# Sixteen experts on one core: 32x32 block turns on VectorE in place of turns on TensorE

## The chip, the cores and the metric

One Trainium2 chip, of which the kernel uses one core. The metric is device microseconds of one execution. All times of the profile are microseconds from the start of its span unless marked ns.

## The reference

One layer over 128 context rows and 512 latent rows, each 1024 wide: a modulated RMSNorm, a mixer (a convolution half and a bidirectional gated linear attention half), an output projection, and then a mixture of experts with a final RMSNorm. The change lies in the mixture, which is:

```python
def _ec_moe(h, w_router, w_gate, w_up, w_down):
    Bn, T, _ = h.shape
    cap = EC_CAPACITY_FACTOR * T // N_EXPERTS          # 64 latent rows, 16 context rows
    probs = jax.nn.softmax((h @ w_router).astype(jnp.float32), axis=-1)
    gates, idx = lax.top_k(jnp.swapaxes(probs, 1, 2), cap)
    xs = h[bidx, idx]
    a = jax.nn.silu(einsum(xs, w_gate)) * einsum(xs, w_up)
    y = einsum(a, w_down) * gates[..., None]
    return jnp.zeros_like(h).at[bidx, idx].add(y)
```

There are 16 experts. Each has three weights of 1024 x 1024 float32 (12.6 MB an expert, 201 MB in all), and takes 64 latent and 16 context rows. Here h is the norm of x2 times (1 + scale2) plus shift2, with one scale and shift for latent rows and one for context rows; then x = x2 + gate2 * mixture, and the final norm. Everything is float32.

## The kernel before

The mixer runs in the first 340 us or so. Then comes the loop over the experts, `expert(e, k)` with k = e on each engine, on which this case turns.

**Weights.** SP (the sync engine) loads each expert in six transfers of 2 MB: u0 and u1 are the first halves of gate and up (512 of the 1024 input rows), u2 and u3 their second halves, u4 and u5 the halves of down. They go through a ring of nine slots (`load_rows`, L552). Transfer n = 6e + u waits until TensorE has used transfer n - 9 (`load_later`, L561: `gu_used` counts two for each expert, `d_used` two). All of them stand in one queue of SP.

**Rows.** POOL gathers an expert's 80 rows of the normalised h from DRAM into `xs` (L675, two buffers) and adds the results of an expert to `sum_l` and `sum_c` in DRAM by indirect DMAs with addition (`add_rows`, L683). The rows of the normalised h are stored so that column j of group kk is input row 4 x partition + j of a weight half.

**TensorE**, for an expert, in this order (L2254): the gate and up products of the 64 latent rows (L2275, `gate_ps` and `up_ps`; it waits for u0 and u1 before the first half and for u2 and u3 before the second, then for the tokens `xT`); the first half of the gate and up products of the 16 context rows (L2305, `ctx_ps`; the pad of 16 columns goes with them); `turn_latent_products` (L2290: the 128x512 tile `act_l` turned in four 128x128 turns into PSUM); the second half of L2305; the latent down products, first half (L2320); `turn_context_products` (L2296: four turns); `turn_tokens(e + 1)` (L2234: the 80x1024 tile `xs` of the next expert in eight turns into pair 2 of PSUM); the second half of L2320; the context down products (L2333).

**ScalarE** takes SiLU of the gate products (L1108 latent, L1112 context) and then brings the turned latent tokens of the next expert from PSUM to `xT` with scale and shift (L1094, eight instructions). **VectorE** multiplies by the up products (L1703, L1710), copies the turned products from PSUM to `aT` (L1706) and `aTc` (L1716), brings the context tokens to `xT` (L1692, L1694), and scales the results into `y_l` and `y_c` (L1698).

**The first expert** has its tokens turned on TensorE in an order of its own (`turn_first_rows`, `first_tokens`).

**The last expert and the end.** While the last expert runs, SP reloads the sums of the other fifteen into `x_sb` (L596, five tiles; the queue is that of the weights). ScalarE squares tiles 0 to 3 (L1103), then does the context SiLU (L1112), loads a table, squares tile 4 and takes the roots (L1120). VectorE, in the order of its program, multiplies tiles 0 and 1 by the gain (`gain_rows`), multiplies `act_c` (L1710), waits for the roots and inverts them (`inverse_after`, L1157 to L1162), copies `aTc` (L1716), finishes rows (`finish_rows`, L1762 and L1765), and only then scales `y_l` (L1698), adds what the other experts left (L1742), and so on. TensorE stops before its last eight context down products for `last_sum_of(0)` (L2251), which needs the squares of that `y_l` (L1135). The last chain goes from `y_c` through L1742, the inverse and L1752 to two scattered stores (L716, L721).

Of the kernel before, what the change touches and what calls it, by code (L numbers as in the profile page):

```python
# [22 lines left out]
ALU = mybir.AluOpType  # L23
# [183 lines left out]
def build(nc, x_prompt, x_sample, s_fwd, s_bwd, c, c_ctx, w_mod, b_mod, g_norm1, g_norm2, w_in, w_conv, b_conv,  # L207
# [3 lines left out]
    with ctx:  # L211
# [9 lines left out]
        def small(name, shape, dt=F32):  # L221
# [86 lines left out]
        xs = at("xs", B_XS, [SLOTS, 2, D])  # L308
# [49 lines left out]
            pool_chain gu_used dl_done d_used xTp_done xT_lat xT_ctx xT_zero gul_done silu_lat silu_ctx act_l_ready  # L358
            act_c_ready aTp_l aTp_c aT_ready aTc_ready yl_ready yc_ready yl_added yc_added sums_in
# [9 lines left out]
         act_chain, pool_chain, gu_used, dl_done, d_used, xTp_done, xT_lat, xT_ctx, xT_zero, gul_done, silu_lat, silu_ctx,  # L369
         act_l_ready, act_c_ready, aTp_l, aTp_c, aT_ready, aTc_ready, yl_ready, yc_ready, yl_added, yc_added, sums_in,  # L370
# [236 lines left out]
        def _(pool):  # L607
# [60 lines left out]
            def gather_first():  # L668

                pool.wait_ge(idx_ready, 2)  # L670
                pool.wait_ge(hn_out[0], 48)
                g.indirect_dma_start(xs[CAP_L:SLOTS, 0, :], None, hn[:, :],
                                     bass.IndirectOffsetOnAxis(ap=first_ctx[0:CAP_C, 0:1], axis=0)).then_inc(xs_ctx, 16)

            def gather(e):  # L675
                if e >= 2:
                    pool.wait_ge(xTp_done, e - 1)
                    pool.wait_ge(xTc_done, 1)
                g.indirect_dma_start(xs[:, e % 2, :], None, hn[:, :],
# [46 lines left out]
        def _(act):  # L726
# [379 lines left out]
            def expert(e, k):  # L1106
                act.wait_ge(gul_done, e + 1)
# [6 lines left out]
                if k < E - 1:  # L1114
                    tokens(e + 1, k + 1)
                else:
# [25 lines left out]
        def _(dve):  # L1142
# [505 lines left out]
            v.memset(xT[:, :, :, SLOTS:96], 0.0).then_inc(xT_zero, 1)  # L1648
# [7 lines left out]
            v.tensor_copy(selr[:, 2, :], pad_rows[:, :])  # L1656
            c = slice(NT - 1, NT)
# [26 lines left out]
            def tokens(e, k):  # L1684
                dve.wait_ge(xT_lat, e + 1)
                if e == 0:
                    dve.wait_ge(xTc_done, 1)
                src = pairs[2][:, :].rearrange("p (b n) -> p b n", b=2)[:, :, 0:4 * SLOTS].rearrange(
                    "p b (k s) -> p b k s", s=SLOTS)[:, :, :, CAP_L:SLOTS]
                dst = xT[:, k % 2, :, CAP_L:SLOTS].rearrange("p (b k) s -> p b k s", b=2)  # L1690
                by = lambda ap: ap.rearrange("p (b k) v -> p b k v", b=2).to_broadcast([P, 2, 4, CAP_C])
                v.tensor_tensor(dst, src, by(scale2[:, :, 1:2]), ALU.mult).then_inc(xT_ctx, 1)  # L1692
                dve.wait_ge(xT_ctx, 2 * e + 1)
# [680 lines left out]
```

## Time and profile before

| | |
|---|---|
| median of 3 runs | 889.68 us (889.63 to 889.81) |
| span of the profiled execution | 889.4 us |
| TensorE (PE) busy | 867.2 us, 98% |
| VectorE (DVE) busy | 286.5 us, 32% |
| ScalarE (ACT) busy | 229.0 us, 26% |
| data moved | 272.39 MB, mean 306 GB/s |

The profiled execution has no time of its own beside its span; the span lies 0.3 us under the median of the runs. In rows of `--timeline` kind the columns are: start, duration (from the first start to the last end of the instructions merged), engine, line, operation, output<-input, shapes, count, and in brackets the idle time before and who ended it. SPq and POOLq are the queues of issues of these engines.

### The profile page before, as it was taken

How to read it: one execution, taken by the hardware profiler on the slowest of the kernel's cores; microseconds unless marked ns; L12 is line 12 of the kernel's file. 1: busy time of each engine (PE TensorE's matmuls, PEld its weight loads, DVE VectorE, ACT ScalarE, POOL GpSimd, SP SyncE). 2: the span in 40 equal slices, each digit the busy share in tenths (PEclk: the TensorE clock that was granted, in tenths of full speed). 3: DMA queues.
4: the chain of work that ended last, by engine and by line, in shares of the span. 5: the costliest groups of instructions: out<-in, count | busy, mean ns of one | idle time of the engine just before them, and what ended most of it. 6: DMA issues, size and time to landing. Idle time of an engine off the chain costs nothing.

```text
span 889.4 us, 14543 instructions
## 1 busy us (share of the span) xinstructions
PE 867.2 (98%) x6341; PEld 480.7 (54%) x6341; DVE 286.5 (32%) x610; ACT 229.0 (26%) x451; POOL 83.2 (9%) x83
## 2 busy tenths in 40 slices
PE   6999999999999999999999999999999999999995
PEld 5798899989998875333333333333333333333332
DVE  3576544777465574201101101101101101101123
ACT  5566634462351333101101101101101101101114
POOL 1000000000000021111011011011011011011013
PEclk9999999999999999999999999999999999999998
DMA  9864714523148358999999999999999999999973
GB/s 329 279 220 165 278 65 136 192 96 134 69 157 349 123 206 303 375 384 410 397 383 412 402 382 409 402 384 409 403 383 415 397 383 412 400 382 410 422 259 135
DMA packets 52770, 272.39 MB, mean 306 GB/s; under 512 B 6378, under 2 KB 16654, under 8 KB 40420
## 3 DMA queue, kind: packets, MB, share of 16 engines
q1 hardware_dynamic: 44908, 255.15, 73.1%
q0 software_dynamic: 6128, 10.89, 5.2%
q10 hardware_dynamic: 1672, 5.43, 1.5%
q8 instruction: 50, 0.82, 0.4%
q14 instruction: 12, 0.10, 0.0%
HBM read 257.95 MB, written 14.55 MB: 306 GB/s over the span
## 4 chain that ended last, share of the span: by engine, by line
PE 91%; DVE 3%; DMA 3%; ACT 1%; SPq 1%; issue 1%; POOLq 0%; POOL 0%; DVEq 0%
PE pair L2275 25%; PE pair L1892 15%; PE pair L2320 13%; PE pair L2305 13%; PE pair L2333 6%; PE pair L2131 5%; PE pair L1832 2%; PE pair L1927 2%; DMA scale_b<-in_w_mod 2%; PE pair L2234 1%; PE pair L2290 1%; DMA p1w<-in_w_out 1%; PE pair L2059 1%; PE pair L2296 1%; PE pair L2050 1%
## 5 line engine op out<-in xcount | busy, mean ns | idle before, releaser
L2275 PE MATMUL pair<-ring,xT 128*64 128x512 f32 x1024 | 223.9, 594 | 0.3 <-ACT xT L1086 0.3
L2275 PEld LDWEIGHTS pair<-ring,xT 128*64 128x64 f32 x1024 | 71.9, 137 | 142.1 <-issue 141.9
L2305 PE MATMUL pair<-ring,xT 128*32 128x512 f32 x1024 | 116.5, 595 | 0.9 <-DVE xT L1694 0.9
L2320 PE MATMUL pair<-ring,aT 128*64 128x512 f32 x512 | 116.9, 598 | 0.0
L1108 ACT ACTIVATE act_l<-pair 128x512 f32<-128x512 f32 x16 | 9.6, 597 | 290.8 <-PE pair L2275 290.8
L1703 DVE TENSOR_TENSOR act_l<-act_l,pair 128x512 f32<-128x512 f32 x16 | 11.0, 687 | 207.9 <-ACT act_l L1108 207.9
L1892 PE MATMUL pair<-hT_hi,w_hi 128*128 128x320 f32 x320 | 75.9, 319 | 0.0
L1892 PE MATMUL pair<-hT_lo,w_hi 128*128 128x320 f32 x320 | 73.1, 310 | 0.0
L1892 PE MATMUL pair<-hT_hi,w_lo 128*128 128x320 f32 x320 | 72.9, 309 | 0.0
L2320 PEld LDWEIGHTS pair<-ring,aT 128*64 128x64 f32 x512 | 34.0, 136 | 69.5 <-issue 68.2
L2305 PEld LDWEIGHTS pair<-ring,xT 128*32 128x32 f32 x1024 | 30.2, 109 | 73.1 <-issue 73.1
L687 POOL DMA_INDIRECT sum_l<-y_l,row_l x15 | 23.4, 1559 | 393.3 <-DVE y_l L1698 393.3
L2333 PE MATMUL pair<-ring,aTc 128*32 128x256 f32 x1024 | 58.8, 381 | 0.0
L1892 PEld LDWEIGHTS pair<-hT_hi,w_hi 128*128 128x128 f32 x320 | 53.0, 188 | 5.7 <-issue 3.9
L1892 PEld LDWEIGHTS pair<-hT_lo,w_hi 128*128 128x128 f32 x320 | 53.7, 188 | 0.0
L1892 PEld LDWEIGHTS pair<-hT_hi,w_lo 128*128 128x128 f32 x320 | 53.7, 188 | 0.0
L1094 ACT ACTIVATE xT<-pair,mod,scale 128x64 f32<-128x64 f32 x120 | 37.2, 412 | 60.9 <-PE pair L2234 60.9
L2333 PEld LDWEIGHTS pair<-ring,aTc 128*32 128x32 f32 x1024 | 31.5, 110 | 32.1 <-issue 13.0
L1234 DVE TENSOR_TENSOR w_lo<-p1w,w_hi 128x1024 fp32r<-128x1024 f32 (+1 forms) x33 | 29.9, 930 | 25.1 <-ACT w_hi L795 24.9
L1112 ACT ACTIVATE act_c<-pair 64x512 f32<-64x512 f32 x16 | 9.4, 589 | 108.8 <-PE pair L2305 108.8
L2131 PE MATMUL pair<-wo_hi,yT_hi 128*128 128x512 f32 x80 | 32.5, 406 | 0.0
L2131 PE MATMUL pair<-wo_hi,yT_lo 128*128 128x512 f32 x80 | 31.6, 395 | 0.0
(307 smaller groups left out, 933.0 us busy)
## 6 DMA issues: line engine op xcount, KB each, us to landing
ring<-in_w_gate SPq DMA_DIRECT2D x32, 2048.0 KB, 30.3
ring<-in_w_up SPq DMA_DIRECT2D x32, 2048.0 KB, 19.4
ring<-in_w_down SPq DMA_DIRECT2D x32, 2048.0 KB, 25.1
p1w<-in_w_mod SPq DMA_DIRECT2D x8, 2048.0 KB, 8.3
p1w<-in_w_in SPq DMA_DIRECT2D x5, 2048.0 KB, 8.0
p1w<-in_w_mod SPq DMA_DIRECT2D x7, 1024.0 KB, 12.3
x_sb<-in_x_sample SPq DMA_DIRECT2D x8, 512.0 KB, 4.9
p1w<-in_w_out SPq DMA_DIRECT2D x2, 2048.0 KB, 8.0
```

The costliest lines, as they stand in the source:

```text
L687: g.indirect_dma_start(rows_l, bass.IndirectOffsetOnAxis(ap=row_l[:, e:e + 1], axis=0), y_l[:, e % 2, :], None, compute_op=ALU.add).then_i ...
L1094: ins = a.activation(xT[:, k % 2, kk, 0:CAP_L], xT_ps(kk)[:, 0:CAP_L], ACT.Identity, bias=mod[:, 3 * KC + kk, 0:1], scale=scale2[:, kk, 0:1])
L1234: v.tensor_tensor(w_lo[place][:, rows, tile(j)], p1w[place][:, rows, tile(j)], rounded(name)[:, rows, tile(j)].bitcast(F32), ALU.subtract) ...
L1703: v.tensor_tensor(in_fours(act_l[:, :]), in_fours(act_l[:, :]), up_ps.rearrange("p (q j) -> p j q", j=4), ALU.mult).then_inc(act_l_ready, 1)
L1832: ins = mm(pp[g:g + 32, 0:mod_width(u)], silu_c[:, k, :], w[:, k, :], start=k < 4, stop=k >= 4)
L1892: ins = mm(pp[:, s * 512:s * 512 + HALF], w, h[:, s * HALF:(s + 1) * HALF], start=k == 0 and i == 0, stop=k == KC - 1 and i == 2)
L1927: ins = mm(pp[:, cols], h, w, start=k == 0 and i == 0, stop=k == KC - 1 and i == 2)
L2131: ins = mm(pp[:, half * 512:(half + 1) * 512], y, w, start=k == 0 and i == 0, stop=k == KC - 1 and i == 2)
L2275: ins = mm(ps[64 * n:64 * n + 64, :], xt[:, kk, 0:CAP_L], w[:, j, n * 512:(n + 1) * 512], start=kk == 0, stop=kk == KC - 1)
L2305: ins = mm(ctx_ps[32 * g:32 * g + 32, :], xt[:, kk, CAP_L:96], w[:, j, n * 512:(n + 1) * 512], start=kk == 0, stop=kk == KC - 1)
L2320: ins = mm(y_ps[0][r:r + 64, :], aT[:, j, 64 * fh:64 * fh + 64], wd[:, j, n * 512:(n + 1) * 512], start=fh == 0 and j == 0, stop=fh == 1 a ...
L2333: ins = mm(y_ps[1][32 * b:32 * b + 32, 0:256], aTc[:, j, 32 * fh:32 * fh + 32], down[fh][:, j, 256 * b:256 * b + 256], start=fh == 0 and j ...
```

## The change

- The eight turns of tokens, for experts 1 to 15, and the four and four turns of products, for all experts, leave TensorE. The helper `turned(dst, src, s, n)` on VectorE does them from SBUF to SBUF: four transposes of 32x32 blocks, one for each output quadrant r, each reading the 32 partitions 32s..32s+31 and writing the 32 partitions 32r..32r+31, n blocks in one instruction.
- Tokens: three times `turned(..., KC)`, 12 instructions of 32x256; `aT`: 16 instructions of 32x128; `aTc`: 8 instructions of 32x128. The copies L1706 and L1716 go. The multiplication before each set is now waited for by VectorE itself.
- The tokens of expert e + 1 are made at the start of expert e on VectorE and ScalarE (for 0 < e < 15), and in expert 0 where they were before. ScalarE's eight instructions now work in place on `xT` in SBUF; VectorE's two for the context rows likewise.
- `xs` has 96 rows, and rows 64 to 95 are cleared once on VectorE (a memset of 32 partitions x 2048) before the first context gather; the memset of `xT` covers one buffer in place of two. POOL's gather of e waits for `xs_turned`, of tokens e - 2.

```diff
@@ gather @@
-                if e >= 2:
-                    pool.wait_ge(xTp_done, e - 1)
+                if e == 2:
+                    pool.wait_ge(xTp_done, 1)
                     pool.wait_ge(xTc_done, 1)
+                if e >= 3:
+                    pool.wait_ge(xs_turned, e - 2)
@@ scalar, tokens and expert @@
-                act.wait_ge(xTp_done, e + 1)
+                act.wait_ge(xs_lat, e)
                 for kk in range(KC):
-                    ins = a.activation(xT[:, k % 2, kk, 0:CAP_L], xT_ps(kk)[:, 0:CAP_L], ACT.Identity,
+                    ins = a.activation(xT[:, k % 2, kk, 0:CAP_L], xT[:, k % 2, kk, 0:CAP_L], ACT.Identity,
             def expert(e, k):
+                if 0 < k < E - 1:
+                    tokens(e + 1, k + 1)
                 act.wait_ge(gul_done, e + 1)
@@ vector @@
-            v.memset(xT[:, :, :, SLOTS:96], 0.0).then_inc(xT_zero, 1)
+            v.memset(xT[:, 0, :, SLOTS:96], 0.0).then_inc(xT_zero, 1)
...
+            v.memset(xs[CAP_L:96, :, :], 0.0).then_inc(xs_zero, 1)
...
+            def turned(dst, src, s, n):
+                for r in range(4):
+                    ins = v.transpose(dst[32 * r:32 * r + 32, :, 32 * s:32 * s + 32],
+                                      src[32 * s:32 * s + 32, :].rearrange("p (k r c) -> p r k c", k=n, r=4)[:, r, :, :])
+                return ins
+            def tokens(e, k):
+                dve.wait_ge(xs_full[k % 2], 16 * (e // 2 + 1))
+                if k >= 2:
+                    dve.wait_ge(gu_used, 2 * (e - 1))
+                turned(xT[:, k % 2], xs[:, k % 2, :], 0, KC)
+                turned(xT[:, k % 2], xs[:, k % 2, :], 1, KC).then_inc(xs_lat, 1)
+                turned(xT[:, k % 2], xs[:, k % 2, :], 2, KC).then_inc(xs_turned, 1)
+                dve.wait_ge(xs_turned, e)
...
             def expert(e, k):
+                if 0 < k < E - 1:
+                    tokens(e + 1, k + 1)
                 dve.wait_ge(silu_lat, e + 1)
...
-                dve.wait_ge(aTp_l, e + 1)
-                v.tensor_copy(aT[:, :, :], gate_ps.rearrange("p (j n) -> p j n", j=4)).then_inc(aT_ready, 1)
+                dve.wait_ge(act_l_ready, e + 1)
+                for s in range(4):
+                    ins = turned(aT, act_l, s, 4)
+                ins.then_inc(aT_ready, 1)
...
-                dve.wait_ge(aTp_c, e + 1)
-                v.tensor_copy(aTc[:, :, :], ctx_ps[:, 0:256].rearrange("p (j n) -> p j n", j=4)).then_inc(aTc_ready, 1)
-                if k < E - 1:
+                dve.wait_ge(act_c_ready, e + 1)
+                for s in range(2):
+                    ins = turned(aTc, act_c, s, 4)
+                ins.then_inc(aTc_ready, 1)
+                if k == 0:
                     tokens(e + 1, k + 1)
@@ tensor, expert @@
-                    if half == 0:
-                        turn_latent_products()
...
-                    if fh == 0:
-                        turn_context_products()
-                        if k < E - 1:
-                            turn_tokens(e + 1, k + 1)
```

## Rows read from the trace of the kernel before

**Rows 1.** Stretches: us; PE, PEld, DVE, ACT, POOL busy; clock; DMA share; GB/s
```profile
700.00:733.50 33.50, 33.50 (x244) 11.85 (x240) 4.31 (x8) 3.67 (x10) 4.04 (x3) 1.00 1.02 399
847.00:855.00 8.00, 8.00 (x41) 2.59 (x37) 1.71 (x5) 0.00 (x0) 1.54 (x1) 1.00 0.58 193
```
**Rows 2.** The chain that ended last, in order of time: start, us, what
```profile
829.99 0.59 PE pair L2290 x4
...
837.73 0.39 PE pair L2296 x4
838.12 0.70 PE pair L2234 x8
...
846.00 13.88 PE pair L2275 x64
```
**Rows 3.** TensorE's timeline: where expert 3 starts
```profile
444.33 7.95 PE L2275 MATMUL pair<-ring,xT 128*64 128x512 f32 x36
```
**Rows 4.** SP's timeline: issues of transfer u3 of experts 3 and 15
```profile
428.45 0.33 SPq L558 DMA_DIRECT2D ring<-in_w_up  x1
830.05 0.33 SPq L558 DMA_DIRECT2D ring<-in_w_up  x1
```
**Rows 5.** Issues by line in two short windows: those two transfers, us to landing last
```profile
ring<-in_w_up SPq DMA_DIRECT2D x1, 2048.0 KB, 16.3
ring<-in_w_up SPq DMA_DIRECT2D x1, 2048.0 KB, 19.5
```
**Rows 6.** Timeline of one middle expert, VectorE and TensorE
```profile
559.36 0.69 DVE L1703 TENSOR_TENSOR act_l<-act_l,pair 128x512 f32<-128x512 f32 x1 [14.01 <-ACT act_l L1108]
566.34 3.65 PE L2320 MATMUL pair<-ring,aT 128*64 128x512 f32 x16
567.10 0.69 DVE L1710 TENSOR_TENSOR act_c<-act_c,pair 64x512 f32<-64x512 f32 x1 [3.53 <-ACT act_c L1112]
```
**Rows 7.** VectorE's timeline before the first expert: a copy, and a wait
```profile
317.36 0.28 DVE L1592 COPY parts<-pair 128x128 f32<-128x128 f32 x1
334.79 0.21 DVE L1656 COPY selr<-pad_rows 16x128 f32<-16x128 f32 x1
336.74 0.16 DVE L1659 TENSOR_TENSOR rms<-rms 128x1 f32<-128x1 f32 x1 [1.74 <-POOL rms L666]
```
**Rows 8.** Groups of VectorE by line: a memset
```profile
L1408 DVE MEMSET states<- 64x512 f32 x1 | 0.5, 485 | 0.0
```
**Rows 9.** Timeline of the end: the reload of the sums and the roots
```profile
854.89 1.76 SPq L596 DMA_DIRECT2D x_sb<-sum_l  x4
862.71 1.06 ACT L1103 ACTIVATE xs_square<-x_sb 128x1024 f32<-128x1024 f32 x1 [2.18 <-DMA x_sb<-sum_l]
867.15 1.06 ACT L1103 ACTIVATE xs_square<-x_sb 128x1024 f32<-128x1024 f32 x1 [0.74 <-DMA x_sb<-sum_l]
871.83 0.19 DVE L1157 RECIPROCAL rms<-rms 128x5 f32<-128x5 f32 x1 [2.20 <-ACT rms L1120]
```
**Rows 10.** Timeline of the end: what follows the roots
```profile
872.65 0.42 DVE L1716 COPY aTc<-pair 128x256 f32<-128x256 f32 x1
873.00 1.27 DVE L1762 SCALAR_TENSOR_TENSOR x_sb<-x_sb,rms,gfin 128x1024 f32<-128x1024 f32 x1
874.19 0.75 DVE L1765 TENSOR_SCALAR x_sb<-final_gain,rms 128x1024 f32<-128x1024 f32 x1
875.10 3.23 PE L2333 MATMUL pair<-ring,aTc 128*32 128x256 f32 x56
875.22 0.75 DVE L1698 SCALAR_TENSOR_TENSOR y_l<-pair,gain,gate_l 128x512 f32<-128x512 f32 x1 [0.29 <-PE pair L2320]
877.34 0.19 ACT L1135 ACTIVATION_READ_ACCUMULATOR left_l<-y_l 128x1 f32 x1
878.26 0.38 PE L2251 MATMUL pair<-last,add_l 128*128 128x1 f32 x2
879.28 0.48 DVE L1698 SCALAR_TENSOR_TENSOR y_c<-pair,gain,gate_c 128x256 f32<-128x256 f32 x1 [2.51 <-PE pair L2333]
```

More of the change, by code:

```diff
@@ L307, in build @@
                 for i, place in enumerate(RING_PLACES)]
-        xs = at("xs", B_XS, [SLOTS, 2, D])
+        xs = at("xs", B_XS, [96, 2, D])
         xT = at("xT", B_XT, [P, 2, KC, 96])
@@ L357, in build @@
             smax_ready probs_ready probsT_ready selr_ready idx_ready wo4_read x2c_ready rootc_ready xrc_ready xs_ctx xTc_done xTp_first xT_first state_out fin_state dve_chain act_chain
-            pool_chain gu_used dl_done d_used xTp_done xT_lat xT_ctx xT_zero gul_done silu_lat silu_ctx act_l_ready
-            act_c_ready aTp_l aTp_c aT_ready aTc_ready yl_ready yc_ready yl_added yc_added sums_in
+            pool_chain gu_used dl_done d_used xTp_done xs_zero xs_lat xs_turned xT_lat xT_ctx xT_zero gul_done silu_lat silu_ctx act_l_ready
+            act_c_ready aT_ready aTc_ready yl_ready yc_ready yl_added yc_added sums_in
             left_in last_added last_ready last_sq last_sum last_root last_out tables_ready pad_ready
@@ L368, in build @@
          exp_ready, smax_ready, probs_ready, probsT_ready, selr_ready, idx_ready, wo4_read, x2c_ready, rootc_ready, xrc_ready, xs_ctx, xTc_done, xTp_first, xT_first, state_out, fin_state, dve_chain,
-         act_chain, pool_chain, gu_used, dl_done, d_used, xTp_done, xT_lat, xT_ctx, xT_zero, gul_done, silu_lat, silu_ctx,
-         act_l_ready, act_c_ready, aTp_l, aTp_c, aT_ready, aTc_ready, yl_ready, yc_ready, yl_added, yc_added, sums_in,
+         act_chain, pool_chain, gu_used, dl_done, d_used, xTp_done, xs_zero, xs_lat, xs_turned, xT_lat, xT_ctx, xT_zero, gul_done, silu_lat, silu_ctx,
+         act_l_ready, act_c_ready, aT_ready, aTc_ready, yl_ready, yc_ready, yl_added, yc_added, sums_in,
          left_in, last_added, last_ready, last_sq, last_sum, last_root, last_out, tables_ready, pad_ready,
@@ L670, in gather_first @@
                 pool.wait_ge(idx_ready, 2)
+                pool.wait_ge(xs_zero, 1)
                 pool.wait_ge(hn_out[0], 48)
@@ L1113, in expert @@
                              ).then_inc(silu_ctx, 1)
-                if k < E - 1:
+                if k == 0:
                     tokens(e + 1, k + 1)
-                else:
+                if k == E - 1:
                     a.activation(smax[:, 0, 0:1], one_col[:, 0:1], ACT.Sqrt)
@@ L1783, in _ @@
             spread(gate_l, gate_c, lambda kind: gate2b[:, kind, :]).then_inc(tables_ready, 1)
-            tokens(0, 0)
+            first_ctx_tokens()
             dve.wait_ge(tables_ready, 1)
@@ L2226, in _ @@
             keep_warm("pTc", 8)
-            def turn_tokens(e, k):
-                pe.wait_ge(xs_full[k % 2], 16 * (e // 2 + 1))
-                if k > 0:
-                    pe.wait_ge(xT_lat, e)
-                    pe.wait_ge(xT_ctx, 2 * e)
-                for kk in range(KC):
-                    ins = turn(xT_ps(kk), xs[:, k % 2, tile(kk)], ident[0:SLOTS, 0:SLOTS])
-                ins.then_inc(xTp_done, 1)
             def turn_first_rows(kk, rows):
@@ L2285, in expert @@
                 pe.wait_ge(xT_ctx, 2 * e + 2)
-                def turn_latent_products():
-                    pe.wait_ge(act_l_ready, e + 1)
-                    for jl in range(4):
-                        ins = turn(gate_ps[:, tile(jl)], act_l[:, tile(jl)], ident[:, :])
-                    ins.then_inc(aTp_l, 1)
-                def turn_context_products():
-                    pe.wait_ge(act_c_ready, e + 1)
-                    for jc in range(4):
-                        ins = turn(ctx_ps[:, 64 * jc:64 * jc + 64], act_c[0:64, tile(jc)], ident[0:64, 0:64])
-                    ins.then_inc(aTp_c, 1)
                 for half in range(2):
```

21 lines of the change are left out of this document (12 added, 9 removed).

## The prediction, made before the changed kernel was run

> **What bounds the kernel now.** I read the stretches first: in one expert's period TensorE is busy for all 33.50 us, VectorE for 4.31 and ScalarE for 3.67, while the DMA share is 1.02 at 399 GB/s [rows 1]. So two things are full at once, and the question is which of them would let the loop run faster. The chain of waits names TensorE alone, and gives the price of what the change takes away: 0.59 us for the four latent turns, 0.39 for the four context turns, 0.70 for the eight token turns [rows 2]. Experts 3 and 15 start at 444.33 and 846.00 [rows 2, 3], so the period is 401.7 / 12 = 33.47 us.
>
> The chain cannot show a transfer that is only just in time, so I set landings against their use. The tightest is u3, the second half of up, which TensorE needs half of 13.88 = 6.94 us after an expert's start. Expert 3: issued at 428.45, landed 16.3 later at 444.75, needed at 451.27: 6.5 us early. Expert 15: issued at 830.05, landed 19.5 later at 849.55, needed at 852.94: 3.4 us early [rows 2 to 5]. The lead fell by 3.1 us in 12 experts. The weight stream thus takes some 33.47 + 0.26 = 33.7 us an expert, already more than TensorE, and TensorE lives on the lead of the ring. At 399 GB/s a 2 MB transfer needs 5.3 us; these took 16 to 20 from issue to landing, so three or four stand in the queue and an earlier issue would land no earlier.
>
> Is it a limit that cannot give? In 847 to 855 the share is 0.58 at 193 GB/s, half of the 16 engines' time unused, yet the reload of the sums, issued at 854.89 behind the last weights in the same queue, let ScalarE start only at 862.71 [rows 1, 9]: 7.8 us for 512 KB. A transfer has landed when its last engine has, and some engines are well behind the others. It is these that set the 33.7; the mean share says little of them.
>
> The end of the kernel is a third thing. VectorE waits for ScalarE's roots, which wait for the fourth reloaded tile at 867.15; it starts its inverse at 871.83 and copies `aTc` at 872.65 [rows 9, 10]. TensorE uses it at 875.10, so that copy is only 2.0 us early (875.10 - 872.65 - 0.42).
>
> **The change part by part.**
>
> *Turns off TensorE.* 16 x (0.59 + 0.39) + 15 x 0.70 = 26.2 us; the period of TensorE alone becomes 33.47 - 1.68 = 31.79.
>
> *Where that goes.* Below the stream's 33.7. TensorE gains 1.68 us an expert on the transfers until the lead is gone (some four experts, 6.5 / 1.9 from expert 3 on) and then waits some 1.5 to 2 us in each expert, mostly for u1 and u3. The late engines have work throughout either way, so I leave the landings where they are. Expert 15 then takes its second half of gate and up at 849.6 in place of 852.9: 3.3 us earlier, and its own turns give 0.98 more, 4.3 in all when TensorE reaches the context down products. Bounds of this term: nothing, if waiting costs more than it looks, and 26.2, if the stream is elastic.
>
> *Turns on VectorE.* No transpose of this kind is in the trace. 32x128: a copy of 128 elements a partition took 0.28 [rows 7]; `aTc`, 256 elements, 0.42 [rows 10]. The lower bound is 0.21, the 128-element copy within SBUF [rows 7]; the upper bound is four times that 0.28, 1.1, if turning were done in several passes. I take 0.28 and 0.42, as the same number of elements is read and written, and hold 0.20 to 0.45 likely for the short one. The Trainium skill (VectorE: DVE Perf Modes, the three transpose paths) gives 311 ns for 128x128 bf16 turned on VectorE; no run here shows it yet, and with it the end below would come 0.24 us later than I say.
>
> - `aT`: 16 x 0.28 = 4.5 us after L1703 ends, against a turn and a copy before. From L1703's start to the use by L2320 there were 566.34 - 559.36 = 6.98 us [rows 6], of which the latent turn's 0.59 goes: 6.39. Needed now: 0.7 + 4.5 = 5.2. Hidden, with 1.2 to spare; it begins to hold TensorE at (6.39 - 0.7) / 16 = 0.36 for one, and to cost time at the end only when that wait is above the 1.9 us that the stream leaves (33.7 - 31.8), at (5.7 + 1.9) / 16 = 0.47.
> - `aTc`: 8 x 0.28 = 2.2 us in place of a turn and 0.42. In a middle expert L1710 ends at 567.8, and the products that read `aTc` start over 6 us later; hidden. Not in expert 15, see below.
> - Tokens: 12 x 0.42 = 5.0, and two of about 0.3, at an expert's start, where VectorE used to wait 14.01 us for L1108 [rows 6]; then ScalarE's eight. They end some 9 us into the expert, and the queue behind them on both engines (L1108, L1703) is not due before 13.9. What they wait for, the gather, was issued a whole expert earlier. In expert 0 the chain aTc, tokens, ScalarE ends about when expert 1 could start; up to 1 us may be late there, and the stream's queue absorbs it, as landings do not hang on it.
>
> *The memset of xs*: 2048 elements a partition. 512 took 0.485 [rows 8], so at most 1.94 us. It stands where VectorE waited 1.74 for POOL [rows 7]; at most 0.2 us comes out, and at the least nothing. It would delay the store of the context rows and the gather of the first context tokens by that. I take 0.1.
>
> *POOL's wait* moves from `xTp_done` to `xs_turned` of two experts before, long fulfilled when it is asked. Issues of SP keep their order; they come up to 4 us earlier into a queue that is full.
>
> *The end, where the cost appears.* The reloaded tiles stand behind the last weights in the late engines' queue, and so does everything up to the inverse: `aTc` can start at 872.65 as before. The program of VectorE then has 8 x 0.28 = 2.24 us of turns: `aTc` ready at 874.9. TensorE, 4.3 us early, would be there at 870.8, and waits: its gain is gone, and L2333 starts at 875.0 where it started at 875.10. Behind the turns VectorE has L1762 and L1765: 1.19 and 0.75 [rows 10], till 876.85. Only then does it scale `y_l`, before at 875.22: 1.6 us later. The squares of `y_l` were ready at 877.53, 2.3 after that start [rows 10], now at 879.2. TensorE needs them for L2251, which ran at 878.26 without waiting for them; now it starts at 879.25, 1.0 later, with the last eight products and `y_c` (879.28 before) behind it. From there the chain is the same. So the end comes 1.0 us later.
>
> *Sum.* Own time of the profiled execution: span 889.4, the median of the runs 0.3 more. 889.4 + 1.0 at the end + 0.1 for the memset = 890.5 of span, 890.8 as a run. With a turn of 0.20: `aTc` ready at 874.25, `y_l` at 876.2, L2251 at 878.6, +0.35. With 0.45: `aTc` 876.25, `y_l` 878.2, L2251 at 880.6, +2.35. The stream's landings are the other unknown, and I give them 2 us towards earlier and 1 towards later; the end follows them one for one, since reload and roots do.
>
> **Rivals.**
>
> 1. *The whole gain is paid out.* TensorE is the bound, the stream follows it: 26.2 us less in the loop. For it: no wait of TensorE for weights in any middle expert. It needs 13.37 MB (399 GB/s x 33.5 us) in 31.8 us, 420 GB/s. Against it: the shrinking lead, and the late engines. Even so the last expert's VectorE could pace the end; about 889.7 - 25 = 865. The Trainium skill (DMA: Bandwidth & Descriptors, Where 436 GB/s comes from) puts the ceiling at 435 GB/s, by which this rival would be allowed; the trace shows mean rates near it, and also that the mean is not what a transfer waits for.
> 2. *The stream comes some us earlier.* The late engines are late partly because slots came free late; earlier issues bring landings and reload 2 to 6 us forward. Then the end is 889.7 + 1.0 - 4 = about 887. For it: at the start of the loop slots come free earlier. Against it: the 16 to 20 us between issue and landing.
> 3. *The turns cost over 0.47 us each (the slower side).* Place: `aT`, between L1703 and L2320, in every expert. At 0.56, twice what I take, they end 9.0 us after L1703, TensorE waits 9.7 - 6.4 = 3.3 us an expert, its period is 35.1, over the stream's 33.7 and 1.6 over the old one: 15 x 1.6 = 24 us, with the roots then long done and nothing more lost at the end: 914. Against it: nothing but that an element a cycle is what every float32 row of VectorE shows. Between 0.40 and 0.47 only the end pays: 891.5 to 892.3.
> 4. *The reload paces nothing.* If the roots come earlier than I think because the fourth tile was late for the gathers of POOL beside it, the end gains 1 us: 889.8.
>
> **Chances.** The forecast with rival 4 and turns up to 0.40: 0.58. Turns of 0.40 to 0.47, or the same end with landings 1 us late: 0.16. Rival 3: 0.05. Rival 2: 0.15. Rival 1 and anything else far down: 0.06. 0.2% of 889.7 is 1.8 us, about what a measurement tells from none: within 887.9 to 891.5 is no change. Most of the first group falls there, the second mostly above, rival 2 mostly below: faster 0.20, no change 0.56, slower 0.24. The range takes in the turn's 0.20 to 0.45, and 2 us of earlier landings and half of rival 2 below: 886.8 to 893.2.
>
> **What would show it.** Right: TensorE's busy share falls by some 3% with its new idle time ended by DMA; L2275 stands idle ahead of u1 and u3 from about expert 5 on; u3 of expert 15 lands within 1 us of 849.6; experts start about 33.5 us apart late in the loop; a transpose of 128 elements takes 0.2 to 0.35; in the last expert TensorE waits for `aTc` ahead of L2333 and L2251 waits for ScalarE. Wrong: expert 15 starts more than 5 us earlier than at 846 (the stream gave), or L2320 is found waiting for `aT` (the turns are dear), or VectorE's inverse starts well before 871.8.

## The result, and the profile after

The changed kernel took 892.5 us (median of 20 runs) against 890.63 (20 runs) for the kernel before on the same chip: ratio 1.0022 [1.0015, 1.0029], 1.9 us slower. The profiled execution of after took 893.77 us with a span of 892.0, 2.6 more than the 889.4 of before. (890.63, not the 889.68 of the table, is what after is to be held against: 0.95 us of the 1.7 between 890.8 and 892.5 is that this chip's runs of before were themselves longer.) The single runs of after spread over 5 us, those of before over 2.

The page of after, parts 1 and 5 (busy us and mean ns of one, idle us in front and its releaser):

```profile
PE 844.1 (95%) x6093; PEld 468.8 (53%) x6093; DVE 463.7 (52%) x1143; ACT 233.1 (26%) x451; POOL 83.3 (9%) x83
...
L2298 PE MATMUL pair<-ring,xT 128*64 128x512 f32 x1024 | 229.8, 602 | 23.0 <-DMA ring<-in_w_up 22.5
...
L1704 DVE STREAM_TRANSPOSE xT<-xs 32x256 f32<-32x256 f32 x180 | 78.2, 434 | 2.6
L1704 DVE STREAM_TRANSPOSE aT<-act_l 32x128 f32<-32x128 f32 x256 | 77.5, 303 | 3.8
...
L1704 DVE STREAM_TRANSPOSE aTc<-act_c 32x128 f32<-32x128 f32 x128 | 38.6, 302 | 2.1
```

A transpose costs about what a copy of as many elements a partition out of PSUM does: 303 ns for 128, 434 for 256, against 0.28 and 0.42 us of the copies [rows 7, 10]. The copy of 128 elements within SBUF took 0.21 [rows 7], and the turn is within SBUF too. Before, TensorE never waited for weights in the loop; now it does for 22.5 us, 11 times. The waits from 345 to 895 us (total us, times, longest):

```profile
PE pair L2298 <- DMA ring<-in_w_up: 22.5, 11, 3.3
```

The stretches of after that answer to [rows 1], eleven periods in one and the end in the others (TensorE, its weight loads, VectorE, ScalarE, POOL; clock; DMA share; GB/s):

```profile
471.00:842.00 371.00, 352.07 (x2475) 122.04 (x2468) 171.41 (x462) 43.42 (x110) 43.48 (x32) 0.99 1.02 399
847.00:855.00 8.00, 5.95 (x30) 2.11 (x28) 0.00 (x0) 0.00 (x0) 0.00 (x0) 1.00 0.71 246
876.00:878.00 2.00, 1.94 (x28) 1.10 (x32) 1.95 (x3) 0.72 (x1) 0.00 (x0) 0.77 0.38 154
878.00:880.00 2.00, 2.00 (x24) 1.05 (x20) 1.44 (x2) 0.40 (x1) 0.00 (x0) 0.50 0.93 375
```

TensorE is idle for 18.9 of 371 us, and the DMA engines do what they did: share 1.02, 399 GB/s. The timeline of the first wait for weights, of a middle expert, and of two stalls after which the same 32 products took longer (start us, busy us, and in brackets the idle time and its releaser), which answers to [rows 3, 6]:

```profile
406.63 13.95 PE L2298 MATMUL pair<-ring,xT 128*64 128x512 f32 x64
...
438.12 7.09 PE L2298 MATMUL pair<-ring,xT 128*64 128x512 f32 x32
446.89 7.09 PE L2298 MATMUL pair<-ring,xT 128*64 128x512 f32 x32 [1.68 <-DMA ring<-in_w_up]
...
455.36 5.05 DVE L1704 STREAM_TRANSPOSE aT<-act_l 32x128 f32<-32x128 f32 x16
460.91 7.09 PE L2329 MATMUL pair<-ring,aT 128*64 128x512 f32 x32
...
471.52 7.09 PE L2298 MATMUL pair<-ring,xT 128*64 128x512 f32 x32
472.06 5.38 DVE L1704 STREAM_TRANSPOSE xT<-xs 32x256 f32<-32x256 f32 x12
...
717.20 8.48 PE L2298 MATMUL pair<-ring,xT 128*64 128x512 f32 x32 [3.32 <-DMA ring<-in_w_up]
...
743.23 14.29 PE L2298 MATMUL pair<-ring,xT 128*64 128x512 f32 x64
...
784.38 8.78 PE L2298 MATMUL pair<-ring,xT 128*64 128x512 f32 x32 [2.23 <-DMA ring<-in_w_up]
```

Experts 2 and 3 start at 406.63 and 438.12, 31.49 us apart: here TensorE still lives on the lead of the ring. In expert 3, at 446.89, the lead is gone and the waits begin, each ahead of the second half of up (u3). Experts 4 and 15 start at 471.52 and 842.31 (next fence): (842.31 - 471.52) / 11 = 33.71 us each. The products on `aT` start at 460.91, without a gap before them; the turns end at 455.36 + 5.05 = 460.41.

The end of after, which answers to [rows 9, 10]:

```profile
842.31 7.09 PE L2298 MATMUL pair<-ring,xT 128*64 128x512 f32 x32
...
851.45 7.09 PE L2298 MATMUL pair<-ring,xT 128*64 128x512 f32 x32 [2.05 <-DMA ring<-in_w_up]
852.09 1.76 SPq L596 DMA_DIRECT2D x_sb<-sum_l  x4
...
863.40 1.06 ACT L1106 ACTIVATE xs_square<-x_sb 128x1024 f32<-128x1024 f32 x1 [4.23 <-DMA x_sb<-sum_l]
...
865.47 7.09 PE L2329 MATMUL pair<-ring,aT 128*64 128x512 f32 x32
...
867.99 1.06 ACT L1106 ACTIVATE xs_square<-x_sb 128x1024 f32<-128x1024 f32 x1
...
872.67 0.19 DVE L1162 RECIPROCAL rms<-rms 128x5 f32<-128x5 f32 x1 [2.20 <-ACT rms L1125]
...
873.49 2.51 DVE L1704 STREAM_TRANSPOSE aTc<-act_c 32x128 f32<-32x128 f32 x8
...
876.06 4.92 PE L2338 MATMUL pair<-ring,aTc 128*32 128x256 f32 x56 [3.50 <-DVE aTc L1704]
...
878.02 0.75 DVE L1724 SCALAR_TENSOR_TENSOR y_l<-pair,gain,gate_l 128x512 f32<-128x512 f32 x1
...
880.13 0.18 ACT L1140 ACTIVATION_READ_ACCUMULATOR left_l<-y_l 128x1 f32 x1
...
880.90 0.38 PE L2274 MATMUL pair<-last,add_l 128*128 128x1 f32 x2
```

TensorE is through with `aT` at 865.47 + 7.09 = 872.56, 2.5 us ahead of the 875.10 at which it read `aTc` before; it waits 3.50 and reads it at 876.06. L2274 (L2251 before) comes at 880.90 in place of 878.26: 2.64 us later, which is the whole difference of the spans. These are two single executions; that of after lay 1.3 us over its median (893.77 and 892.5).

### The profile page after: what moved, and what is told of

It reads as the page before. It is cut to its first block, busy times and chain, and to the rows that moved or that the text cites. A ratio compares the mean times of both kernels' runs of the same rounds, so it can differ in the third digit from the quotient of the medians.

```text
span 892.0 us, 14566 instructions
## 1 busy us (share of the span) xinstructions
PE 844.1 (95%) x6093; PEld 468.8 (53%) x6093; DVE 463.7 (52%) x1143; ACT 233.1 (26%) x451; POOL 83.3 (9%) x83
## 4 chain that ended last, share of the span: by engine, by line
issue 35%; PE 35%; DMA 22%; DVE 5%; ACT 2%; ACTq 0%; POOLq 0%; SPq 0%; POOL 0%; DVEq 0%
DMA sum_l<-y_l,row_l 20%; PE pair L1924 15%; PE pair L2163 5%; PE pair L1864 2%; PE pair L1959 2%; DMA x_sb<-sum_l 2%; PE pair L2298 2%; PE pair L1971 1%; DMA p1w<-in_w_out 1%; PE pair L1903 1%; PE pair L2091 1%; PE pair L2316 1%; PE pair L2338 1%; PE pair L2082 1%; PE pair L1873 1%
## 5 line engine op out<-in xcount | busy, mean ns | idle before, releaser
L2298 PE MATMUL pair<-ring,xT 128*64 128x512 f32 x1024 | 229.8, 602 | 23.0 <-DMA ring<-in_w_up 22.5
L2298 PEld LDWEIGHTS pair<-ring,xT 128*64 128x64 f32 x1024 | 77.2, 138 | 165.4 <-issue 164.7
L2316 PE MATMUL pair<-ring,xT 128*32 128x512 f32 x1024 | 113.2, 594 | 0.9 <-DVE xT L1699 0.9
L2329 PE MATMUL pair<-ring,aT 128*64 128x512 f32 x512 | 113.4, 595 | 0.0
L1097 ACT ACTIVATE xT<-xT,mod,scale 128x64 f32<-128x64 f32 x120 | 41.4, 427 | 193.6 <-DVE xT L1704 193.6
L1704 DVE STREAM_TRANSPOSE xT<-xs 32x256 f32<-32x256 f32 x180 | 78.2, 434 | 2.6
L1704 DVE STREAM_TRANSPOSE aT<-act_l 32x128 f32<-32x128 f32 x256 | 77.5, 303 | 3.8
L2316 PEld LDWEIGHTS pair<-ring,xT 128*32 128x32 f32 x1024 | 32.0, 110 | 79.7 <-issue 79.7
L2338 PEld LDWEIGHTS pair<-ring,aTc 128*32 128x32 f32 x1024 | 32.2, 112 | 36.6 <-issue 13.8
L1704 DVE STREAM_TRANSPOSE aTc<-act_c 32x128 f32<-32x128 f32 x128 | 38.6, 302 | 2.1
```

Source lines behind the costliest of these rows:

```text
L1097: ins = a.activation(xT[:, k % 2, kk, 0:CAP_L], xT[:, k % 2, kk, 0:CAP_L], ACT.Identity, bias=mod[:, 3 * KC + kk, 0:1], scale=scale2[:, kk ...
L1704: ins = v.transpose(dst[32 * r:32 * r + 32, :, 32 * s:32 * s + 32], src[32 * s:32 * s + 32, :].rearrange("p (k r c) -> p r k c", k=n, r=4) ...
L2298: ins = mm(ps[64 * n:64 * n + 64, :], xt[:, kk, 0:CAP_L], w[:, j, n * 512:(n + 1) * 512], start=kk == 0, stop=kk == KC - 1)
L2316: ins = mm(ctx_ps[32 * g:32 * g + 32, :], xt[:, kk, CAP_L:96], w[:, j, n * 512:(n + 1) * 512], start=kk == 0, stop=kk == KC - 1)
L2329: ins = mm(y_ps[0][r:r + 64, :], aT[:, j, 64 * fh:64 * fh + 64], wd[:, j, n * 512:(n + 1) * 512], start=fh == 0 and j == 0, stop=fh == 1 a ...
L2338: ins = mm(y_ps[1][32 * b:32 * b + 32, 0:256], aTc[:, j, 32 * fh:32 * fh + 32], down[fh][:, j, 256 * b:256 * b + 256], start=fh == 0 and j ...
```

## The experiments

Ratios are against the kernel before on the same chip; it ran at 890.6 to 890.7 us in each set. After was not run again in these sets; differences to it are taken from its 892.5, and by the ratios they come out within 0.6 us of that. A timeline is that of one execution, and landings move by a us or two between executions; what a variant is worth is read from the medians.

**1. Turns of the last `aTc` ahead of the roots** (in after):

```diff
-                if k == E - 1:
-                    dve.wait_ge(froot_ready, 1)
-                    inverse_after(rms, slice(0, NT), rms[:, 0, :], finv_ready)
                 ... (turns of act_c into aTc)
+                if k == E - 1:
+                    dve.wait_ge(froot_ready, 1)
+                    inverse_after(rms, slice(0, NT), rms[:, 0, :], finv_ready)
```

> The changed kernel, but in the last expert VectorE turns aTc before it waits for the roots and inverts them. Theory (the loop is paced by the landing of weights, and the loss is made at the end by turns that wait behind the roots): act_c is multiplied about 870.5, aTc ready about 873.0 instead of 876.0, TensorE's context down products start 3 us earlier and its clock is not lowered by the 3.5 us stall; the squares of y_l then pace L2274, at 878.6 instead of 880.9. 2 to 3 us less than the changed kernel: 889.5 to 890.5. Rival (the loss is made in the loop, by turns that TensorE waits for): no difference to the changed kernel, 892.5.

889.35 us (12 runs), 0.9988 [0.9979, 0.9997]: 3.15 us below after, and 0.15 below the expected range. Its timeline at the end:

```profile
868.20 2.51 DVE L1704 STREAM_TRANSPOSE aTc<-act_c 32x128 f32<-32x128 f32 x8
...
870.76 3.23 PE L2338 MATMUL pair<-ring,aTc 128*32 128x256 f32 x56 [0.56 <-DVE aTc L1704]
...
876.00 0.35 PE L2274 MATMUL pair<-last,add_l 128*128 128x1 f32 x2 [2.00 <-ACT left_l L1140]
```

One change of order in VectorE's last program takes away the whole loss of after and 1.3 us more. As expected, L2274 waits for the squares of `y_l` here (2.00 us). With 0.56 us of waiting in front, the same 56 products take 3.23 us and not 4.92.

**2. The rest of the end ordered too** (experiment 1, and: ScalarE does the SiLU of the context rows after two of the five tiles, and the squares of `y_l` ahead of its third row copy; VectorE scales `y_l` ahead of `finish_rows`):

```diff
-                    final_squares(0, 4)
+                    final_squares(0, 2)
                 ... (SiLU of act_c)
+                    final_squares(2, 4)
...
+                        if t == 4:
+                            last_square(0)
...
-                if k == E - 1:
-                    finish_rows()
                 ... (y_l)
+                    finish_rows()
```

> As the kernel that turns aTc first, and also in the last expert: ScalarE does the context SiLU after two squares instead of four, VectorE scales y_l before it finishes rows 2 and 3, and ScalarE squares that y_l before its third copy of rows. Theory: everything behind the roots leaves TensorE's path, y_c is scaled about 877.6 instead of 881.9, and then the store of the finished rows (done about 881) is what the last scattered store waits for: 887.5 to 889, below the kernel before. Rival (loss in the loop): 892.

888.24 us (6 runs), 0.9971 [0.9959, 0.9982]. This beats both kernels: 2.4 us below before, 4.3 below after. Its timeline:

```profile
850.64 7.09 PE L2305 MATMUL pair<-ring,xT 128*64 128x512 f32 x32 [2.36 <-DMA ring<-in_w_up]
...
871.68 3.23 PE L2345 MATMUL pair<-ring,aTc 128*32 128x256 f32 x56
...
876.39 0.48 DVE L1732 SCALAR_TENSOR_TENSOR y_c<-pair,gain,gate_c 128x256 f32<-128x256 f32 x1 [0.53 <-PE pair L2345]
...
880.78 1.01 POOL L719 DMA_INDIRECT out<-y_l,row_l  x1 [8.79 <-DMA out<-x_sb]
```

`y_c` is scaled 2.9 us earlier than before (879.28, [rows 10]), but the last store of results now waits for the stores of the other rows: from here the reload paces the end.

**3. TensorE kept as busy as before** (after, with the 16 turns of an expert issued as turns of the identity that nobody reads):

```diff
+                    if half == 0:
+                        for jl in range(4):
+                            turn(sc_ps[:, tile(jl)], ident[:, :], ident[:, :])
...
+                    if fh == 0:
+                        for jc in range(4):
+                            turn(sc_ps[:, 64 * jc:64 * jc + 64], ident[0:64, :], ident[0:64, 0:64])
+                        if k < E - 1:
+                            for kk in range(KC):
+                                turn(sc_ps[:, 80 * (kk % 6):80 * (kk % 6) + 80], ident[0:80, :], ident[0:80, 0:80])
```

> The changed kernel with the sixteen turns of each expert left on TensorE as well, of the identity into an unused part of PSUM, so that TensorE has the work of before (33.5 us an expert) and VectorE that of after. Theory (weights pace the loop): TensorE's turns fill time in which it would wait for weights, so the same within 0.5 us as the changed kernel, 892 to 893. Rival (the turns removed did bring their 26 us, and VectorE's turns or a slower stream took them back): 10 to 26 us more, 903 to 918.

893.12 us (11 runs, 0.1 over the expected range), 1.003 [1.0021, 1.0038], against 1.0022 [1.0015, 1.0029] of after. The loop as one stretch, first with the idle turns:

```profile
377.00:845.00 468.00, 468.00 (x3362) 165.43 (x3358) 218.18 (x588) 55.26 (x140) 55.96 (x42) 1.00 1.01 399
```

and in experiment 1, where TensorE has 14 experts' turns less in it:

```profile
377.00:845.00 468.00, 448.89 (x3150) 154.64 (x3148) 218.95 (x591) 55.27 (x140) 57.23 (x43) 0.99 1.02 399
```

TensorE idles for 19.1 us or not at all, both move 399 GB/s, and the time is the same to within the intervals. Here TensorE comes to `aTc` late and waits little, so its clock holds:

```profile
875.22 3.23 PE L2347 MATMUL pair<-ring,aTc 128*32 128x256 f32 x56 [0.98 <-DVE aTc L1704]
879.62 0.35 PE L2274 MATMUL pair<-last,add_l 128*128 128x1 f32 x2 [1.18 <-ACT left_l L1140]
```

**4. Only the tokens on VectorE** (products turned by TensorE and copied as before):

```diff
-                for s in range(2):
-                    ins = turned(aTc, act_c, s, 4)
-                ins.then_inc(aTc_ready, 1)
+                dve.wait_ge(aTp, 2 * e + 2)
+                v.tensor_copy(aTc[:, :, :], ctx_ps[:, 0:256].rearrange("p (j n) -> p j n", j=4)).then_inc(aTc_ready, 1)
```

(and the same for `aT`, with the two groups of turns back in TensorE's program.)

> Only the tokens are turned on VectorE; the products are turned on TensorE and copied as before. TensorE's period is 32.8 us without waits. Theory: the loop is still paced by the landings, so nothing of the 10.5 us of token turns comes back; at the end TensorE waits a little for act_c (870.5) and starts the context down products at about 874.6 instead of 875.1: 889 to 890.5, the kernel before within 1 us. Rival (TensorE paces the loop): 879 to 881.

890.43 us (12 runs), 0.9993 [0.9984, 1.0001]. With the products turned on TensorE again the loss is gone; the token turns' 0.7 us an expert are hidden by the stream: TensorE waits 7.5 us for weights, 8 times.

**5 and 6. A lighter stream** under before and under after. From expert 2 on only 512 of the 1024 columns of each half of down are loaded, so the products read stale weights:

```diff
+                if e >= 2 and u >= 4:
+                    sp.dma_start(ring[n % TURNS][:, :, 0:512], src[:, 0:512].rearrange("(p k) n -> p k n", p=P)
+                                 ).then_inc(w_full[n % TURNS], 16)
+                    return
```

> The kernel before, but from expert 2 on only the first 512 of the 1024 columns of w_down are loaded (the products use what the slots held), so that an expert's weights are 10.5 MB in place of 12.6 and the stream's 33.7 us become about 28.5, less than TensorE needs. Theory: TensorE paces this kernel with or without that, so nearly nothing changes: 888 to 891.

> The changed kernel with the same half loads of w_down from expert 2 on. Theory (the landings of weights hide the turns' removal): now the 1.68 us an expert come out, 13 to 15 times, less what the end gives back: 22 to 26 us below the kernel before with the same loads, 864 to 869. Rival (VectorE's turns hold TensorE in the loop, or the loop is bound elsewhere): within 3 us of that kernel.

Before: 890.72 us (10 runs), 1.0001 [0.9992, 1.001]: nothing. After: 860.24 (4 runs), 0.9662 [0.9648, 0.9677], 30.5 us below the one beside it and 3.8 below the lower end of what was expected. Two expert starts in the lightened after:

```profile
720.46 13.95 PE L2302 MATMUL pair<-ring,xT 128*64 128x512 f32 x64
...
751.95 13.96 PE L2302 MATMUL pair<-ring,xT 128*64 128x512 f32 x64
```

The period is 31.49 us, as between experts 2 and 3 of after itself, and 1.98 under the 33.47 of before, where the turns' rows sum to 1.68. The other 0.30 is what a turn in the middle of a group costs the products around it: they go in two halves of 3.57 us each with a turn between them ([rows 6] and the trace of experiment 12: 725.88 to 729.45, 730.04 to 733.61), and in one run of 7.00 without (734.34 to 741.34 here), 0.14 an interruption, two an expert. So TensorE was given back some 30 us, not 26, and all of it is there to be had once the stream is light.

**7, 10 and 12. What makes the stream slow: the adds.** In 7 (on after) and 12 (on before) the adds of results are left out for experts 1 to 13, in 10 (on after) only the context rows' adds. The edit of 7:

```diff
+                if e not in (0, E - 2):
+                    return
-                    pool.wait_ge(yl_added, 16 * e)
+                    pool.wait_ge(yl_added, 16)
...
-                    sp.wait_ge(yl_added, 16 * (E - 1))
+                    sp.wait_ge(yl_added, 32)
```

(the counts waited for in the other places follow.)

> The changed kernel with the adds of results to DRAM left out for experts 1 to 13 (those of 0 and 14 stay), all weights loaded. It asks what makes some DMA engines late. If it is the software queue's share beside the weights (8.5% of the engines' time, some three quarters of it adds), the stream takes about 31.5 us an expert and TensorE (31.8) becomes the bound: 865 to 872. If the lateness is of the weight transfers' own, the stream keeps most of its 33.5: 885 to 892.

864.21 us (4 runs), 0.9698 [0.9683, 0.9713], 28.3 below after and 0.8 below the lower end of what was expected. Its loop as one stretch:

```profile
471.00:800.00 329.00, 326.78 (x2292) 113.12 (x2290) 160.82 (x433) 42.22 (x108) 8.08 (x9) 1.00 1.01 410
```

Its waits for weights (total us, times, longest):

```profile
PE pair L2300 <- DMA ring<-in_w_up: 2.2, 3, 1.1
```

Its software queue in 700 to 733.5 us (packets, MB, share of the 16 engines' time):

```profile
q0 software_dynamic: 96, 0.33, 3.2%
```

In after, in the same stretch:

```profile
q0 software_dynamic: 384, 0.66, 8.5%
```

The adds take 5.3 points of the engines' time. Without them a period of 33.7 us should need 33.7 x 0.947 = 31.9; experts start 31.77 apart (724.83 and 756.60). The two agree, but TensorE's own 31.49 of experiment 6 is so near that the stream's bound may lie lower still. A third of a megabyte an expert (0.66 - 0.33), in small packets, costs nearly as much as TensorE had to gain.

> The changed kernel with only the adds of context results left out for experts 1 to 13; the latent adds stay. Each is one indirect DMA of 128 rows with addition, of 1 KB against 2 KB. If the adds cost the late engines by rows, this gives half of what leaving out both gave, or more: the stream falls from about 33.5 to 32.5 us an expert, 876 to 880. If by bytes, a third: 882 to 885. If the context rows, half of which are pads that are skipped, cost nothing: 892.

881.4 us (4 runs), 0.9894 [0.9879, 0.9908]: 11.1 of the 28.3 us, 39%, between the two branches (by rows, by bytes). The software queue's share fell only from 8.5 to 7.2%; by the arithmetic above that is 0.44 us an expert, 5.7 us in 13. What gives the other 5 is not shown, so the share of time is not the whole price of an add.

> The kernel before with the adds left out for experts 1 to 13, the partner of the changed kernel with the same adds left out (864.2). Theory (before, TensorE's 33.5 us an expert are the bound and the adds cost it nothing; only once TensorE's turns are gone do the adds decide): 889.5 to 891. Rival (the adds cost any version of the kernel time): 865 to 875.

889.03 us (10 runs), 0.9982 [0.9972, 0.9992], just under the expected range; the rival with the stream as the bound of before is out by 14 us or more. Its experts start at 712.00 and 745.46, 33.46 apart, at 387 GB/s. With the same load taken off the stream, before gains 1.6 us and after 28.3: TensorE bounded the loop before, the stream bounds it after, and the two bounds lay 0.25 us an expert apart.

**8 and 11. The same order of the end in the kernel before.** 8 has the edits of experiment 2 in ScalarE's program and `aTc` copied ahead of the inverse (`finish_rows` stays ahead of `y_l`); 11 adds the reload of the sums on ScalarE's own queue. 8's edit in VectorE's program:

```diff
+                dve.wait_ge(aTp_c, e + 1)
+                v.tensor_copy(aTc[:, :, :], ctx_ps[:, 0:256].rearrange("p (j n) -> p j n", j=4)).then_inc(aTc_ready, 1)
                 ... (wait for the roots, and the inverse)
-                dve.wait_ge(aTp_c, e + 1)
-                v.tensor_copy(aTc[:, :, :], ctx_ps[:, 0:256].rearrange("p (j n) -> p j n", j=4)).then_inc(aTc_ready, 1)
```

> The kernel before with the order of the end of the fast variant (context SiLU after two squares, aTc copied ahead of the inverse, the squares of y_l ahead of the third copy of rows; the finished rows stay ahead of y_l). It asks whether the variant's 2.4 us come from the order alone. Theory: here TensorE itself paces the end, and waits for none of these: the kernel before within 0.5 us, 890.2 to 891.2. Rival (the order alone pays): 888.

892.0 us (11 runs), 1.0015 [1.0006, 1.0024]: a miss, 1.4 us slower where the same to within 0.5 us was expected.

> The kernel before with the edits of the end of the variant before it (reload on ScalarE's queue, context SiLU after two squares, aTc copied ahead of the inverse, squares of y_l ahead of the third copy of rows). It asks whether the turns on VectorE are of any use to the best variant. Theory: TensorE paces this kernel to its end: the kernel before within 0.8 us, 889.8 to 891. Rival (the end order and the reload alone pay): 887.

892.15 us (11 runs), 1.002 [1.0011, 1.0028]: also a miss, and no sign of the 887 of the rival. A row of experiment 8's timeline, ScalarE's SiLU of the context rows:

```profile
866.53 0.59 ACT L1118 ACTIVATE act_c<-pair 64x512 f32<-64x512 f32 x1 [1.96 <-PE pair L2313]
```

TensorE is through with the products in front at 866.40 here and at 864.66 in experiment 2, so a SiLU that stands after the second tile waits for it, and the remaining tiles and the roots with it. That is a reading of one profiled execution, which was also the fastest of the 11 (890.53), so the median's 1.4 us is not explained by it; why it is slower stays open. What the two runs do show: these edits of the order alone give before nothing. That experiment 2's gain needs TensorE to be early is the likely reading; `y_l` ahead of `finish_rows`, which experiment 2 also has, was not tried in before.

**9. The reload on another queue** (experiment 2, with the sums read back by ScalarE's queue in place of SP's):

```diff
-                sp.dma_start(x_sb[:, t, :], sum_l[tile(t), :] if t < NT - 1 else sum_c[0:P, :]).then_inc(sums_back[t], 16)
...
+                        act.dma_start(x_sb[:, t, :], sum_l[tile(t), :] if t < NT - 1 else sum_c[0:P, :]).then_inc(sums_back[t], 16)
```

> The fast variant (turns on VectorE, end reordered), and the reload of the sums is issued by ScalarE at the start of the last expert, on its own queue, instead of by SP behind the last weights. Theory (a transfer waits for engines that are behind with the weights ahead of it in its queue; the end then waits for the stores of the finished rows): the tiles land some 5 us earlier, the roots and the row stores with them, u4 and u5 land later but are not due; then TensorE alone sets the end from the landing of u3 on: 886 to 887.5, 1 to 2 us below the fast variant. Rival (the reload was not what the row stores waited for, or the weights are delayed as much): 888 to 890.

889.74 us (12 runs), 0.9993 [0.9983, 1.0004]: a miss, 1.5 us above experiment 2 and inside the rival's 888 to 890. Its timeline:

```profile
852.46 1.78 ACTq L1118 DMA_DIRECT2D x_sb<-sum_l  x4
...
862.76 1.06 ACT L1099 ACTIVATE xs_square<-x_sb 128x1024 f32<-128x1024 f32 x1 [3.08 <-DMA x_sb<-sum_l]
...
865.73 1.06 ACT L1099 ACTIVATE xs_square<-x_sb 128x1024 f32<-128x1024 f32 x1 [1.81 <-DMA x_sb<-sum_l]
```

The reload was issued no earlier than in experiment 2:

```profile
851.28 1.76 SPq L596 DMA_DIRECT2D x_sb<-sum_l  x4
```

In both it first waits until the latent results of expert 14 have been added to the sums (`yl_added`), and so it did before, where SP stood for 20.3 us:

```profile
SPq L593 <- DMA sum_l<-y_l,row_l: 20.3, 1, 20.3
```

So the tiles could not land 5 us earlier, and what an earlier reload would give is not tested. From issue to landing the five transfers took 10.3 to 14.6 us here (median 12.9) and 11.3 to 13.8 in experiment 2 (median 13.0): a queue of their own gained them next to nothing beside the weights. ScalarE's program now holds the waits for the adds too, until 858.71 for those of the context rows (the issue of `sum_c`, which is not among the rows shown); whether that is why the median is 1.5 us worse is not shown.

## Why the prediction was right, and where it was short

The forecast was 1.1 us slower than before (890.8 against 889.7) and the medians on one chip say 1.9. The time is inside the range, but not in the class that got the most (0.56 for a change of less than 1.8 us): it lies just over its edge. The errors at the end add up, they do not cancel.

*The loop is paced by landings, and the gain becomes idle time: right.* L2298 is idle for 22.5 us for weights, expert 15 starts 3.7 us earlier (846.00 to 842.31), and the period is 33.71 us against the 33.7 worked out from the shrinking lead. Experiment 3 shows it from the other side: 19 us of TensorE's time, given or withheld, change nothing. Experiments 6 and 7 against 5 and 12 show which bound holds in which kernel. The waits were all ahead of u3, none ahead of u1, and began in expert 3 and not 5: TensorE's 1.98 us an expert had used up the lead by then (expert 3 starts 6.2 us earlier than before, of a lead of 6.5). Rival 1 was out for this kernel; without the adds the stream came down to 31.77 us an expert, at 410 GB/s. The Trainium skill (DMA: Bandwidth & Descriptors, Where 436 GB/s comes from) puts the ceiling at 435 GB/s; the loops here mean 399 to 410 and do not test it as a limit. Its sentence there that the HBM side, some 358 GB/s a core, binds a load from HBM does not hold for these loads of a single core.

*Why a landing is late: half right.* The prediction blamed engines that are well behind the others. In the loop the time share of the software queue is enough to account for most of it (8.5 to 3.2%, 33.7 to 31.9 us), whichever engines it falls on; experiment 10 fits this less well. The Trainium skill (DMA: Bandwidth & Descriptors, Latency and other measured facts) says that two of the 16 engines are usually slower, with the software queue's rings as its guess; that this queue's traffic is dear agrees (28.3 us for 13 experts' adds), which engines it falls on no run here shows.

*u3 of expert 15: 1.8 us later than said.* It landed at 828.40 + 22.9 = 851.3 (issue row and its time to landing), where 849.55 was kept and 1 us allowed; TensorE went on at 851.45. Experiments 1, 2 and 9 have TensorE going on there at 849.1 to 851.8, so this is within the spread of single executions. That the end now hangs on landings all the way is a likely reason why the single runs of after spread more; no run tests it. It follows that TensorE was 1.5 + 1.0 = 2.5 us early at `aTc`, not 4.3; as it waited for VectorE, this cost nothing.

*What the turns give TensorE: mis-sized.* 1.98 us an expert, not 1.68 (experiment 6). Adding up the turns' own rows missed the 0.14 us by which each group of turns split the products around it.

*Price of a turn: right, a little low.* 303 ns for 0.28 and 434 for 0.42; eight in a row took 2.51 us and not 2.24, so 0.27 more at the end. The Trainium skill's 311 ns for a turn of bf16 (VectorE: DVE Perf Modes, The three transpose paths) is within 3% of the float32 row, and its 0.24 us was the better guess. TensorE never stood idle for `aT`, whose turns end before the products in front do; rival 3 is out.

*The end: the mechanism right, 1.0 us taken, 2.64 measured in the profiled execution.* Three steps of that part were off.

- "`aTc` can start at 872.65 as before": the inverse came at 872.67 and not 871.83, +0.84. The reload was issued 2.8 us earlier than before (852.09 for 854.89), and yet its first tile was used 0.7 us later (863.40 for 862.71). The prediction named only the weights in front of the reload; what holds its issue is the add of expert 14's results (experiment 9). In experiments 1 and 3, where ScalarE's program up to the roots is that of after, the inverse came at 870.74 and 870.75, so the 0.84 is within the spread of single executions and not shown to be a cost of the change.
- "8 x 0.28": the turns took 0.27 more. Both delays pass through `finish_rows` and `y_l` as written, and the squares of `y_l` were ready at 880.31 in place of the predicted 879.2.
- "L2333 starts at 875.0" and, from it, "now it starts at 879.25" of L2251: this counted when TensorE would start and not how fast it would run after its wait. After standing idle for 3.50 us TensorE ran at the 1.2 GHz level (granted clock 0.50 in 878 to 880), so the 56 products took 4.92 us in place of 3.23 and were done only at 880.9, 0.6 after the squares. L2274 did not wait for ScalarE, as the prediction's signs had it, but for TensorE itself. Before, the clock in the same 2 us was 1.00:

```profile
878.00:880.00 2.00, 1.21 (x18) 0.46 (x10) 0.61 (x2) 0.26 (x1) 0.00 (x0) 1.00 1.01 397
```

Together, 1.0 + 0.84 + 0.27 + 0.6 = 2.7, against 2.64. Without the 0.84 some 1.9 is left, which is what the medians differ by (892.5 - 890.63); that is an estimate, as one execution of after was profiled. With TensorE kept busy (experiment 3) the clock held and L2274 came at 879.62. Of the 1.28 us between that and 880.90, 0.84 is that the turns of `aTc` began at 872.65 there and not at 873.49, and some 0.45 is the clock. The medians do not show this 0.45: that of experiment 3 is 893.12. Turned first (experiment 1) L2274 came at 876.00.

*The memset:* 0.13 us for 0.1.

*Rival 2* (the stream comes earlier) was out: u3 was not earlier. *Rival 4* was out too; the roots came later, not earlier.

## What to carry to other kernels

When two resources are full at once, take load off each alone, in both versions: 1.6 and 28.3 us for the same adds left out say at once which one binds where. An engine relieved below the other bound only gets idle time, and that can cost: move its new waits to where nothing hangs on them, and look at what is queued behind a longer instruction in the last iteration, since with the turns ahead of the roots the same kernel is faster than before and not slower. Small accumulating transfers cost far more than their bytes: 0.33 MB of 13 an expert, 5.3 points of the engines' time, 28.3 us. Even their share of the time is no full price (experiment 10: 5.7 us by it, 11.1 measured). And before a transfer is moved to another queue, look at what its issue waits for.

## What the runs showed of the hardware

- In after, TensorE's clock stood at its half level (1.2 GHz) after idle stretches of 3.32, 3.50 and once of 2.23 us: the 32 products at 717.20 took 8.48 us and those at 784.38 8.78 for 7.09, the 56 at 876.06 took 4.92 for 3.23. Behind its other waits, of 1.62 to 2.09 us, they took 7.09. In all the kernels with turns on VectorE the products kept their 7.09 us behind waits of up to 2.11 us, were slower behind some and not behind others of 2.15 to 2.53 (8.79 us behind 2.15 in experiment 2, 7.09 behind 2.49 in experiment 1), and were slower behind every one of 2.76 and more. In the loop of after this cost nothing that could be seen: the expert behind a slow one started its 64 products and did not wait for weights at all (743.23), so the lost time stood in place of a wait.
- VectorE turns 32x128 float32 in 303 ns and 32x256 in 434, SBUF to SBUF, as long as a copy out of PSUM; a copy of 128 elements within SBUF took 0.21 us.
- The adds of 13 experts, by the software queue, cost a kernel that the stream bounds 28.3 us, those of the context rows alone 11.1; a kernel that TensorE bounds, 1.6 us.
- Transfers issued on ScalarE's queue took about as long from issue to landing as behind the weights on SP's (median 12.9 and 13.0 us).
